# Weight slots that climb with the moving tile: the place of the first two slots of a group in a one-core mLSTM and attention block

## What is computed

```
proj = rmsnorm(x) @ w_in               # q, k, v, o, z, two gates, u, zb, ga, gb
qk   = silu(causal_conv(q, k));  h = mlstm_chunkwise(q, k, v, gates)
y_a  = sigmoid(o) * norm(h) * silu(z);   y_b = pool_mix(u) * silu(zb)
m    = sigmoid(ga) * (y_a @ w_proj_mlstm) + sigmoid(gb) * (y_b @ w_proj_pool)
x    = x + rmsnorm(m @ w_out)          # end of the first block
h    = concat(16 meta tokens, x)       # second block: differential and latent
out  = rmsnorm(h + attention(h) @ w_out_2)[16:]    # attention, 8 heads each
```

## Time and profile before

| | |
|---|---|
| median of 3 runs | 1461.4 us (1460.16 to 1461.64) |
| the profiled execution | 1462.16 us, of which the span is 1460.5 us |
| granted TensorE clock, mean over the span | 0.995 |
| TensorE busy | 1435.6 us, 98% |
| VectorE, ScalarE busy | 850.6 us, 707.5 us |
| matmuls | 10878 |

### The profile page before, as it was taken

The page is one execution under the profiler, slowest core; times in us unless marked ns, Lnnn a source line. Parts: engine busy times, 40 slices in busy tenths (PEclk is TensorE's granted clock), DMA queues, the critical chain, the costliest instruction groups (busy, mean ns, idle before and its releaser), DMA issues.

```text
span 1460.5 us, 27819 instructions
## 1 busy us (share of the span) xinstructions
PE 1435.6 (98%) x10878; PEld 1370.6 (94%) x10878; DVE 850.6 (58%) x1054; ACT 707.5 (48%) x929; POOL 63.1 (4%) x95
## 2 busy tenths in 40 slices
PE   6999999999999999999999999999999999999997
PEld 6999998899999999999999999888999999999786
DVE  5676674546655666545454545556555545667754
ACT  5545544545555444434344444446433346667543
POOL 0000000001110000000000000001000002111000
PEclk8999999999999999999999999999999999999999
DMA  6655645655555555555655556656555553334553
GB/s 228 201 190 184 201 166 192 196 178 177 168 175 193 175 186 190 174 194 182 199 189 191 193 190 214 247 173 217 203 172 169 178 174 121 121 121 136 208 198 122
DMA packets 71940, 266.01 MB, mean 182 GB/s; under 512 B 8088, under 2 KB 8096, under 8 KB 70944
## 3 DMA queue, kind: packets, MB, share of 16 engines
q1 hardware_dynamic: 69840, 253.12, 51.9%
q0 software_dynamic: 1440, 10.63, 2.1%
q10 hardware_dynamic: 576, 1.05, 0.2%
HBM read 260.56 MB, written 4.20 MB: 181 GB/s over the span
## 4 chain that ended last, share of the span: by engine, by line
PE 93%; DVE 3%; ACT 1%; DVEq 1%; issue 1%; DMA 0%; ACTq 0%; POOL 0%; SPq 0%; POOLq 0%
PE ps L350 23%; PE ps L354 22%; PE ps L352 22%; PE ps L342 6%; PE ps L343 6%; PE ps L344 6%; PE ps L462 2%; DVE wl L1220 1%; DVEq L1215 1%; PE ps L748 1%; PE ps L540 1%; PE ps L551 1%; DMA xn<-in_x 0%; PE ps L589 0%; ACT wh L900 0%
## 5 line engine op out<-in xcount | busy, mean ns | idle before, releaser
L1220 DVE TENSOR_TENSOR wl<-raw,wh 128x1024 fp32r<-128x1024 f32 x474 | 580.0, 1227 | 501.1 <-ACT wh L900 492.6
L900 ACT ACTIVATE wh<-raw 128x1024 fp32r<-128x1024 f32 x474 | 499.9, 1060 | 555.9 <-PE ps L354 426.7
L350 PE MATMUL ps<-xh,wh 128*128 128x256 f32 x1792 | 499.7, 279 | 3.0 <-DVE xl L1229 1.8
L352 PE MATMUL ps<-xl,wh 128*128 128x256 f32 x1792 | 498.0, 278 | 0.0
L354 PE MATMUL ps<-xh,wl 128*128 128x256 f32 x1792 | 497.9, 278 | 0.0
L350 PEld LDWEIGHTS ps<-xh,wh 128*128 128x128 f32 x1792 | 337.9, 189 | 3.7 <-DVE xl L1229 2.2
L352 PEld LDWEIGHTS ps<-xl,wh 128*128 128x128 f32 x1792 | 338.1, 189 | 0.1
L354 PEld LDWEIGHTS ps<-xh,wl 128*128 128x128 f32 x1792 | 338.0, 189 | 0.0
L350 PE MATMUL ps<-x2h,wh 128*128 128x256 f32 (+1 forms) x688 | 199.2, 290 | 1.0 <-DVE avt L1387 0.4
L354 PE MATMUL ps<-x2h,wl 128*128 128x256 f32 (+1 forms) x688 | 194.8, 283 | 0.0
L352 PE MATMUL ps<-x2l,wh 128*128 128x256 f32 (+1 forms) x688 | 194.5, 283 | 0.0
(11 more groups left out here) (337 smaller groups left out, 1772.8 us busy)
## 6 DMA issues: line engine op xcount, KB each, us to landing
raw<-in_w_stream SPq DMA_DIRECT2D x474, 512.0 KB, 3.3
xn<-in_x SPq DMA_DIRECT2D x4, 512.0 KB, 7.7
xr<-in_x POOLq DMA_DIRECT2D x1, 2048.0 KB, 12.3
x_kept<-xr POOLq DMA_DIRECT2D x1, 2048.0 KB, 9.1
x1r<-x_kept POOLq DMA_DIRECT2D x1, 2048.0 KB, 10.0
mrow<-bound_rows POOLq DMA_DIRECT2D x8, 128.0 KB, 3.5
poolw<-in_pool_w POOLq DMA_DIRECT2D x1, 1024.0 KB, 6.3
postw<-in_post_w POOLq DMA_DIRECT2D x1, 1024.0 KB, 5.2
```

Source lines behind the costliest of these rows:

```text
L350: pe.matmul(out_at(j), whr[:, c, f], hi(kc)[:, tokens], start=st, stop=False, skip_group_check=True)
L352: pe.matmul(out_at(j), whr[:, c, f], lo(kc)[:, tokens], start=False, stop=False, skip_group_check=True)
L900: act.activation(slot_view(wh_at[r], layout), raw[r][:, :, :], ACT.Copy).then_inc(wh_done, 1)
L1220: tt(slot_view(wl_at[r], layout), raw[r][:, :, :], slot_view(wh_at[r], layout).bitcast(F32), ALU.subtract).then_inc(split_done, 1)
```

## The change

A new list, `FOLLOWS`, gives the first two slots of a group the layouts (48, 516) and (56, 516): their four chunks begin at words 48, 52, 56 and 60 modulo 64 instead of 0. It applies to kinds whose layout is `ON_RAMP`, except in the groups of `BEGINS` and in all of OZ. That leaves seven QK groups, zb of UZ 1, all of MG but its first ga. V and WO now copy their first three layouts from round 1 of the stage before, which is what the loop writes; so their first two slots have the new layouts too, the third stays at (0, 512). No instruction is added or removed.

```diff
+FOLLOWS = ((48, 516), (56, 516))
+BEGINS = {("QK", 0, 0), ("UZ", 0, 0), ("UZ", 0, 1), ("UZ", 1, 0), ("MG", 0, 0)}
+
+
 def slot_layouts():
 
-    out, last = [], []
+    def layout(name, i, j, kind, k):
+        begins = name == "OZ" or (name, i, j) in BEGINS
+        if LAYOUT_OF.get(kind) == ON_RAMP and not begins and k < len(FOLLOWS):
+            return FOLLOWS[k]
+        return LAYOUT_OF.get(kind, BY_FEATURE)
+
+    out, looped = [], []
     for name, kinds, times in STAGES:
-        of = [LAYOUT_OF.get(kind, BY_FEATURE) for kind in kinds for _ in range(slots_of(kind))] * times
+        of = [layout(name, i, j, kind, k) for i in range(times) for j, kind in enumerate(kinds)
+              for k in range(slots_of(kind))]
         if name in ("V", "WO"):
-            of[:LEAD] = last[:LEAD]
+            of[:LEAD] = looped
+        per = len(of) // times
+        looped = of[per:per + LEAD]
         out += of
-        last = of
     return out
```

## The result

The changed kernel takes 1475.26 us against 1461.14 us in the same session, a ratio of 1.0096 with an interval of 1.0076 to 1.0116: 14 us slower, where 4 us less were forecast. The two profiled executions, 1475.22 and 1462.16 us, are 13.1 us apart, and so are their spans, 1473.6 and 1460.5; the groups are compared in these two. QK 0,1 starts at 45.91 after and at 45.92 before, so nothing is lost ahead of it. One execution of the changed kernel (1786.33 us) and one of a later one, with y and z flat (1787.89 us), ran at a mean granted clock of 0.75 and stand outside the ratios.

What follows compares the result with a forecast made beforehand. TensorE's matmul count times pace was taken as the bound. Gains of 4.75 us in 19 groups, less 0.4 for pb and 0.1 for WO, gave -4.2 on the 1461.4 median: 1457.2 us, 80% range 1456.0 to 1471.5.

Steps and rivals of the forecast that it cites:

- What bounds the kernel: TensorE, busy 98% of the span: time is the number of matmuls times their pace, with the splits running ahead.
- Lead 16 has two paces, and the pace is inherited: At lead 16 (moving chunk's start minus weights', in words) matmuls take 113.3 or 117.7 ns, as the group was entered.
- part (2): New single-matmul steps, lead 12 four times inside a group and 32 at its edge, taken to cost 0 if survived.
- fast pace everywhere: The sum's assumption that groups run at 113.3 ns; 19 groups then gain 0.25 us each, 4.75 in all.
- R3: Rival, chance 0.13: the lead 32 at the group's edge breaks the pace in 19 groups, 0.60 us each; +11.9, 1473.3 us.
- R1: Rival, chance 0.20: slow pace is inherited by 7 QK groups and, behind pb, by three MG rounds; +9.4, 1470.8 us.
- pb: Four MG groups whose lead becomes 32 at once: +0.09 us each, +0.4 together; bounds -0.15 and +0.17 each.
- WO: First two slots, moved from lead 0 to 48 to 60: +0.1 us, between 0 and +0.2.
- V: First slots, with the lead becoming 48 in all six chunks: 0 taken, between -0.2 and +0.1 us.
- the splits: Rows written 516 apart instead of 512: VectorE could lose 0.01 us in 46 slots, hidden; 0.5 us if uncovered.
- The rule weighed there: Two independent SBUF read ports, read as addresses not mattering and the change worth nothing; the prediction said the trace disagrees.

Runs made afterwards that it cites:

- flat-tile kernel: Kernel before with activations unramped, every chunk at lead 16; weights' places make leads 0, 4, 8, 12 behind other work: 1479.85 us, 1.0117 times before.
- fourth kernel of steps: Kernel before, ramps kept, chosen groups moved: QK 0,1 and QK 1,1 by 0 words, zb by 8, gb of MG 0 by -16, later ga and gb by -8: 1467.48 us.
- steps_a: Flat-tile kernel without the weights' ramp in chosen groups, which are moved for one edge matmul at lead 32, 12, 20 or 0: 1480.99 us.
- steps_b: As steps_a with other moves: one edge matmul at lead 12, 32, 8 or 48, and a four-chunk climb in QK 1,1: 1480.51 us.
- steps_c: Kernel before, ramps kept, chosen groups moved: lead 24 into QK 0,1, 32 into QK 1,1, climb in zb, no step or 12 into gb, ga straight: 1465.79 us.
- qk_straight: Kernel before with y and z flat, and QK rounds 1 to 3 reading an unramped copy of x's first four chunks: 1456.46 us, ratio 0.9969.
- ramp_8: Kernel before with the ramp of xh and xl cut to leads 8, 12, then 16, and z without ramp: 1477.98 us.
- ramp_0: Kernel before with the ramp of xh and xl cut to one chunk at lead 0, then 16, and z without ramp: 1478.37 us.
- last two kernels: Kernel before with y and z flat, 1459.35 us (ratio 0.9984), and the same with an unramped copy of x for QK rounds 1 to 3, 1456.46 us (0.9969).

## Why the prediction was wrong

It said 1457.2 us and up to 1471.5; it was 1475.26. Point by point:

- **What bounds the kernel** held: matmuls times pace; splits stayed ahead; no wait changed sides.
- **Lead 16 has two paces, and the pace is inherited** held too (a third, 118.3 to 118.4 ns, was seen where weights and tile are moved by 4 words), and became the strongest result: in the flat-tile kernel the slow one passes through seven step-free groups, in the fourth kernel of steps the fast one through QK 1,1.
- **The failed step is the price of the new steps in part (2)**, "I take 0 for a step that survives", and with it the sum's "fast pace everywhere". The steps neither keep a fast pace nor mend a slow one. From fast, a single 32 costs QK 1,1 0.85 us (22.61 against 21.76 step-free), and a single 12 is enough too; from slow, 32, 12 and the climb leave it slow (steps_a, steps_b). The sum needed the second as well, since QK 0,0 hands on a slow pace. The 0 rested on one matmul at lead 0 in a gate group, another stage with another distance between its places, and that row was read as if it spoke for a step of 32. It is also the only one of the four gate groups whose slot 6 is fast in that trace; the others are slow from their start, and so say nothing of what the step costs. The only row with a 32 in it was known to show both outcomes. R3 named the step and the 19 groups, and came with 0.13 and "nothing speaks against it but" that same row; it was left outside the range. The row that was the nearest in form (a short step at lead 16) was farthest in kind: the same name, a single matmul at another lead, covered two different moves of the two reads.
- **Its size.** R3's 0.60 a group was 0.63, 12.1 against 11.4 in all; the rest is mostly slots 0 and 1, which run at 118.2 to 118.4 ns instead of 117.7. Whether the single matmuls at lead 12 do that or the places themselves isn't shown.
- **R1**, with 0.20 and inside the range, was right in its mechanism and accounts for most of the loss: its 16 groups (7 QK, and ga, pa, gb of three rounds) were entered slow, and groups entered slow without a step stay slow, in QK (flat tile) as behind pb (steps_c). What it leaves out are zb of UZ 1 and pa and gb of MG 0, which it took to gain 0.25 us each: two were entered fast and lost the pace at the edge, gb inherited it. These three make 2.7 of the 4.5 us that R1's 1470.8 lacks; of the changed kernel's own groups only they tell R3 from R1.
- **pb**: +0.5 against +0.4. Slots 0 and 1 ran at 119.0 ns, not at the 118.3 of lead 32 two slots on, within the bounds given.
- **WO**: +0.64 against +0.1. This is a misread diff, and the section on the change misses it too. WO's first three slots were priced as a loop's tail; that every WO group gets the new layouts by the equality of two tuples was overlooked, and the experiment that takes it back returns 0.5 of it; the 0.13 that stay are the +0.1 that was priced. V was 0, as said; the splits too.
- The rule weighed there: at equal leads and equal shapes the distance is 113.3 or 117.8 ns, depending on where the two reads lay before. The Trainium skill, "TensorE: Matmul & The Clock Gate", "Step-by-step: what each phase is for", says that PE has two independent SBUF read ports. That places wouldn't matter was drawn from it in the prediction, and this is what the runs contradict; the ports themselves no run here shows.

**Still open.** Why a step loses the pace, and why the tile's ramp restores it where the same leads made by the weights don't, isn't shown by a profile that has only starts. Lead 24 took slow to fast in two groups, fast to slow in three of one kernel, and did nothing in another; which of these happens isn't settled. The ramp's smallest sure form isn't known either. Copies without a ramp for ga, gb and zb weren't tried. In the first block only steps over leads 32, 24, 12 and 8 were tried from the fast pace; the 0 of the earlier trace rows wasn't. The ratio's 14.1 us against 13.1 in the profiles is within what the profiled execution of before stood above its median.

## What to carry to other kernels

Where the same instructions run at two paces, look first for what the pace depends on: history can be part of it, and then a change in two slots is paid or earned in all that follow. Read the pace from the distance of starts at a point that the edit doesn't touch. A price read at one step holds for that step: a 0 was free where it was measured, a 32 and a 12 cost 0.85 us and more a group. A tuned beginning that looks like a cost of 0.25 us may be what sets the state for the other 144 matmuls; remove it only where a trace shows the state handed on without it, as for pb, pa and QK here.

## What the runs showed of the hardware

- Matmuls of 256 float32 columns with a weight load each run at 113.3 or 117.8 ns from start to start, at the same lead of 16 words, at a granted clock of 0.995 to 0.998 (the 2.4 GHz level) in all these runs. Neither passes into the other by itself in 192 matmuls, nor over step-free edges between groups (slow: seven QK groups of the flat tile; fast: six of qk_straight). Where weights and tile are both moved by 4 words, lead 16 gave 118.3 to 118.4 ns.
- In the first block the fast pace was lost each time that weights and tile moved together: with the climb and the 32 (zb and the first pa of the changed kernel), over a single 32 (four groups), a single 24 or 12 (three groups each) or 8 (one), and in the climb alone. It isn't so everywhere: in slot 6 of G 1 both move by 16 words, over one matmul at lead 0, and it runs on at 113.2 ns.
- With the weights in place it survived a low chunk of the tile at 12 (21.82 us a group) and was lost over 8, 12 or a single 0 (gb of ramp_8 and ramp_0, 22.62 and 22.64 us).
- The beginning varies: QK 0,1 starts between 43.35 and 46.78 us in these profiles, so two spans are compared only behind it. That is 2.2 of the 3.2 us between the spans of the last two kernels (1458.0 and 1454.8 us).
- The Trainium skill, "TensorE: Matmul & The Clock Gate", "Back-to-back issue gap", gives N / 2.4 + 2.5 ns as the gap of an isolated matmul at the 2.4 GHz level, by estimate 109.2 ns for 256 columns. No run here shows it: with a weight load for each matmul, the best is 113.3.
